# Forgetting-attention decay and mask added on VectorE instead of TensorE; sample output computed with the probabilities stationary, its jobs moved inside the latent-attention heads

## The reference

```python
def _fox_block(q, fq, qpos, k, v, fk, kpos):
    logits = jnp.einsum('bqhd,bkhd->bhqk', q, k, ...) * FOX_SCALE
    decay = jnp.swapaxes(fq, 1, 2)[..., :, None] - jnp.swapaxes(fk, 1, 2)[..., None, :]
    mask = kpos[None, :] <= qpos[:, None]
    p = jax.nn.softmax(jnp.where(mask, logits + decay, NEG_INF), axis=-1)
    return jnp.einsum('bhqk,bkhd->bqhd', p.astype(v.dtype), v)
...
    F = jnp.cumsum(logf_all, axis=1)
...
    o = o.reshape(B, T, FOX_WIDTH) * jax.nn.silu(gate)
    return x + o @ w_out, (k, v, logf.astype(x.dtype))
...
def _mla_block(qn, qr, qpos, kn, kr, v, kpos):
    logits = (einsum(qn, kn) + einsum(qr, kr)) * MLA_SCALE
    mask = (kpos // CHUNK)[None, :] <= (qpos // CHUNK)[:, None]
    p = jax.nn.softmax(jnp.where(mask, logits, NEG_INF), axis=-1)
    return jnp.einsum('bhqk,bkhd->bqhd', p.astype(v.dtype), v)
```

## Time and profile before

| | us |
|---|---|
| median of 3 runs | 2469.4 |
| lowest and highest | 2463.78, 2470.36 |
| the profiled execution | 2464.83 |
| its span, first to last instruction | 2462.8 |
| mean granted TensorE clock | 0.981 of full speed |
| PE busy | 2320.0 (94%) |
| DVE busy | 1099.7 (45%) |
| ACT busy | 910.0 (37%) |
| POOL busy | 212.9 (9%) |

### The profile page before, as it was taken

One profiled execution on the slowest core, in us unless ns is written; L12 is line 12 of the kernel. 1 busy time (PEld: TensorE's weight loads), 2 busy tenths in 40 slices (PEclk: granted clock), 3 DMA queues, 4 the chain that ended last, 5 costly groups with the idle time before them and its releaser, 6 DMA issues. The chain is left out here.

```text
span 2462.8 us, 34026 instructions
## 1 busy us (share of the span) xinstructions
PE 2320.0 (94%) x12338; PEld 1962.2 (80%) x12338; DVE 1099.7 (45%) x2361; ACT 910.0 (37%) x1947; POOL 212.9 (9%) x189
## 2 busy tenths in 40 slices
PE   3899999999999999999997999997699999997998
PEld 2788888888888888877886978887689989996887
DVE  4244444444444444444223343224566666664322
ACT  5233334434333334343223332224444444443211
POOL 0000000000000000000000000004721111110000
PEclk9999999999999999999999999998999999998999
DMA  2322222222222222223433222223321111113332
GB/s 85 103 87 78 86 86 73 82 86 85 79 86 83 81 86 78 87 78 100 159 99 106 74 90 102 100 88 100 127 92 43 47 51 51 43 40 116 120 119 73
DMA packets 95535, 212.33 MB, mean 86 GB/s; under 512 B 9504, under 2 KB 38432, under 8 KB 94768
## 3 DMA queue, kind: packets, MB, share of 16 engines
q1 hardware_dynamic: 95472, 211.45, 26.8%
HBM read 178.60 MB, written 32.82 MB: 86 GB/s over the span
## 5 line engine op out<-in xcount | busy, mean ns | idle before, releaser
L215 PE MATMUL bank<-b_whi,x_hi 128*128 128x512 f32 x1024 | 414.0, 404 | 12.7 <-DVE b_wlo L198 12.7
L215 PE MATMUL bank<-b_wlo,x_hi 128*128 128x512 f32 x1024 | 401.0, 392 | 0.0
L215 PE MATMUL bank<-b_whi,x_lo 128*128 128x512 f32 x1024 | 400.8, 391 | 0.0
L198 DVE SCALAR_TENSOR_TENSOR b_wlo<-b_raw,g_fox,b_whi 128x512 fp32r<-128x512 f32 x256 | 180.9, 748 | 186.1 <-ACT b_whi L185 186.1
L215 PEld LDWEIGHTS bank<-b_whi,x_hi 128*128 128x128 f32 x1024 | 192.8, 188 | 52.2 <-DVE b_wlo L198 12.8
L185 ACT ACTIVATE b_whi<-b_raw,g_fox 128x512 fp32r<-128x512 f32 x256 | 170.6, 715 | 171.4 <-PE bank L215 157.4
L215 PEld LDWEIGHTS bank<-b_whi,x_lo 128*128 128x128 f32 x1024 | 192.6, 188 | 42.3
L215 PEld LDWEIGHTS bank<-b_wlo,x_hi 128*128 128x128 f32 x1024 | 193.0, 188 | 33.8
L215 PE MATMUL bank<-m_whi,x_hi 128*128 128x512 f32 x320 | 124.9, 390 | 0.8 <-DVE m_wlo L198 0.8
L215 PE MATMUL bank<-m_wlo,x_hi 128*128 128x512 f32 x320 | 124.6, 389 | 0.0
L215 PE MATMUL bank<-m_whi,x_lo 128*128 128x512 f32 x320 | 124.5, 389 | 0.0
(11 more groups left out here) (490 smaller groups left out, 5232.2 us busy)
## 6 DMA issues: line engine op xcount, KB each, us to landing
b_raw<-w_fox SPq DMA_DIRECT2D x128, 512.0 KB, 3.5
m_raw<-w_mla SPq DMA_DIRECT2D x40, 512.0 KB, 3.4
c_raw<-w_out SPq DMA_DIRECT2D x32, 512.0 KB, 3.5
g_raw<-w_out SPq DMA_DIRECT2D x32, 512.0 KB, 3.5
f_raw<-w_ukv SPq DMA_DIRECT2D x16, 512.0 KB, 3.4
queries<-e_q SPq DMA_DIRECT2D x16, 480.0 KB, 3.4
f_q<-queries SPq DMA_DIRECT2D x16, 480.0 KB, 3.4
e_raw<-w_uq SPq DMA_DIRECT2D x16, 384.0 KB, 3.5
```

Source lines behind the costliest of these rows:

```text
L198: op = eng.scalar_tensor_tensor(lo[:, k, :], raw[:, k, :], self.gain[:, K:K + 1], hi32[:, k, :], ALU.mult, ALU.subtract)
L215: op = eng.matmul(out, a, w[:, k, :], start=(first and k == 0 and i == 0), stop=(last and k == self.kk - 1 and i == len(pairs) - 1))
```

## The change: what it does, and its diff

**FoX scores.** The two extra products of each score job go. Block a negates F of all heads (DVE), and stores it in a new DRAM tensor `decay`. For each head, SP loads row h of it into five tiles, each row repeated on all partitions (128, 256, 384 and 512 columns on 128 partitions, 576 columns on 64), and POOL adds the mask to the diagonal part of each. DVE's maximum becomes a `tensor_tensor_reduce`: it adds the decay tile to the scores in PSUM, writes the negated sum back, and keeps the minimum. ACT's exponential takes scale -1. A memset of one element stands ahead of each.

**Sample output, both layers.** v is stored as hi and lo side by side, and so are the transposed sample probabilities. One matmul for each key tile holds hi and lo of the probabilities stationary (128 columns) and moves hi and lo of v (256 columns), so 5 matmuls; the fifth has zeros in the lower 64 rows. The result has four parts: ACT copies the lower 64 partitions out, DVE adds twice and multiplies with the gate as it is, and the new job ont transposes that; ACT copies it to the output. Job gn goes.

**Order.** In FoX: before g, gn, o, on in slots 30, 31, 33, 35; after g, o, on, ont in slots 30, 32, 34, 37. In MLA as in the diff.

```diff
-            dve.wait_ge(f_hi.sem, 3)
-            dve.tensor_tensor(K.B[32:32 + HEADS, :], F[:], K.B[0:HEADS, :].bitcast(F32), ALU.subtract).then_inc(f_lo.sem, 1)
...
+            dve.tensor_scalar(nF[:], F[:], -1.0, None, ALU.mult).then_inc(f_neg.sem, 1)
...
+            sp.dma_start(d["decay"], nF[:]).then_inc(out.sem, 16)
...
-            self.sel.wait(eng, g, 2)
             q = slice(i * P, (i + 1) * P)
             for m, (x, y) in enumerate(three(self.qhi, self.qlo, self.khi, self.klo)):
-                eng.matmul(b[:, 0:n], x[:, q], y[:, 0:n], start=(m == 0), stop=False)
-            eng.matmul(b[:, q], K.ident_b[:, :], K.mask_fox_b[:, :], start=False, stop=False, skip_group_check=True)
-            op = eng.matmul(b[:, 0:n], K.A[:, q], K.B[:, 0:n], start=False, stop=True)
+                op = eng.matmul(b[:, 0:n], x[:, q], y[:, 0:n], start=(m == 0), stop=(m == 2))
...
+        self.decay_masked.wait(eng, g, TT)
+        k = ("s0", "s1", "s2", "s3", "sa", "sb").index(name)
+        eng.memset(self.mark[:, k:k + 1], 0.0)
...
-            eng.tensor_reduce(self.nm[:, i:i + 1], b[:, 0:(i + 1) * P], AX.X, ALU.max, negate=True).then_inc(self.negmax.sem, 1)
+            x = b[:, 0:(i + 1) * P]
+            eng.tensor_tensor_reduce(x, x, self.decay[i][:], -1.0, BIG, ALU.add, ALU.min,
+                                     accum_out=self.nm[:, i:i + 1]).then_inc(self.negmax.sem, 1)
...
+                    if g is not None:
+                        H.negmax.wait(sp, g, TT)
+                    row = d["decay"][bass.ds(h, 1)] if not isinstance(h, int) else d["decay"][h:h + 1]
+                    for i in range(NT):
+                        n = (i + 1) * P
+                        sp.dma_start(H.decay[i][:], row[:, 0:n].broadcast_to([P, n])).then_inc(H.decay_in.sem, 16)
+                    sp.dma_start(H.decay_new[:], row[:, SEQ:].broadcast_to([NEW, SAMP])).then_inc(H.decay_in.sem, 16)
...
             def head(g):
...
-                pool.tensor_copy(K.A[0:64, :], K.nsel[0:64, bass.ds(g, 1)].broadcast_to([64, SEQ + NEW])).then_inc(H.sel.sem, 1)
...
+                H.decay_in.wait(pool, g, TT)
+                for i in range(NT):
+                    x = H.decay[i][:, i * P:]
+                    pool.tensor_tensor(x, x, K.mask_fox[:], ALU.add).then_inc(H.decay_masked.sem, 1)
...
                 H.var.wait(pool, g, 1)
                 pool.tensor_tensor(H.rstd[:], H.ss[:], H.half[:], ALU.pow).then_inc(H.rst.sem, 1)
...
         elif name == "on":
+            self.v_lo.wait(eng, g, TT)
             for t in range(TT):
-                n = rows(t)
-                for m, (x, y) in enumerate(three(self.vhi, self.vlo, *self.ptn)):
-                    op = eng.matmul(b[:, 0:256], x[0:n, NT + t, :], y[0:n, t * NEW:t * NEW + 256],
-                                    start=(t == 0 and m == 0), stop=(t == SM and m == 2))
+                op = eng.matmul(b[:, 0:256], self.ptn[:, t, :, :].rearrange("p a q -> p (a q)"),
+                                self.v[:, NT + t, :, :].rearrange("p a d -> p (a d)"), start=(t == 0), stop=(t == SM))
...
+            self.on_moved.wait(eng, g, 1)
+            src = b[0:NEW, 0:256].rearrange("p (a d) -> p a d", a=2)
+            self.release(eng.tensor_tensor(self.on_sum[:], src, self.on_lo[:], ALU.add), name)
+            self.wait_out_of(eng, g, name)
+            eng.tensor_tensor(self.on[:], self.on_sum[:, 0, :], self.on_sum[:, 1, :], ALU.add).then_inc(self.on_added.sem, 1)
+            self.on_added.wait(eng, g, 1)
+            eng.tensor_tensor(self.on[:], self.on[:], self.gate[0:NEW, SM, :], ALU.mult).then_inc(self.on_added.sem, 2)
...
     ORDER = ["qn", "kp", "qr", "T0", "T1", "s3", "ka", "T2", "s2", "new", "T3", "s1", "s0", "T8", "sa", "sb", "T4",
-             "p3", "T5", "p2", "p1", "p0", "T6", "pn", "g", "gn", "T7", "on", "o"]
+             "p3", "T5", "pn", "p2", "p1", "T6", "on", "p0", "g", "T7", "ont", "o"]
```

More of the change, by code:

```diff
@@ L305, in block_a @@
     F = place("a_F", [HEADS, TIME])
+    nF = place("a_nF", [HEADS, TIME])
     T = Transposer(c, "a", x, act, K.ident, KT)
@@ L310, in block_a @@
     wf_hi, wf_lo, f_mm, f_mv, f_sum = c.sem("a_wf_hi"), c.sem("a_wf_lo"), c.sem("a_f_mm"), c.sem("a_f_mv"), c.sem("a_f_sum")
-    soft, logs, scan, f_hi, f_lo, f_t, f_tc, out = (c.sem(f"a_{n}") for n in
-        ("soft", "logs", "scan", "f_hi", "f_lo", "f_t", "f_tc", "out"))
+    soft, logs, scan, f_neg, f_t, f_tc, out = (c.sem(f"a_{n}") for n in
+        ("soft", "logs", "scan", "f_neg", "f_t", "f_tc", "out"))
     with nc.Block() as block:
@@ L371, in _ @@
             act_.activation(e[:], e[:], ACT.Exp).then_inc(soft.sem, 1)
-            act_.wait_ge(soft.sem, 3)
+            act_.wait_ge(soft.sem, 1)
             act_.activation(e[:], e[:], ACT.Ln, bias=K.one_col[0:HEADS, :]).then_inc(soft.sem, 1)
[L375 to L379, removed]
         @block.vector
@@ L803, in pe_job @@
                 op = eng.transpose(b[:, t * P:(t + 1) * P], self.gate[:, t, :], K.ident[:, :])
-        elif name == "gn":
-            op = turn(eng, b[:, 0:NEW], self.gate[0:NEW, SM, :], K.ident[0:NEW, 0:NEW], True)
+        elif name == "ont":
+            self.on_added.wait(eng, g, 3)
+            op = turn(eng, b[:, 0:NEW], self.on[:], K.ident[0:NEW, 0:NEW], True)
         self.end(op, name)
@@ L1953, in pe_job @@
                 f = self.first[j]
-                for m, (x, y) in enumerate(three(self.vhi, self.vlo, *self.pt[j])):
-                    op = eng.matmul(b[:, f:], x[:, j, :], y[:, :], start=(j == 0 and m == 0), stop=(j == NT - 1 and m == 2))
+                for m, (x, y) in enumerate(three(self.v[:, j, 0, :], self.v[:, j, 1, :], *self.pt[j])):
+                    op = eng.matmul(b[:, f:], x, y[:, :], start=(j == 0 and m == 0), stop=(j == NT - 1 and m == 2))
         elif name == "on":
+            self.v_lo.wait(eng, g, TT)
             for t in range(TT):
-                n = rows(t)
-                for m, (x, y) in enumerate(three(self.vhi, self.vlo, *self.ptn)):
-                    op = eng.matmul(b[:, 0:256], x[0:n, NT + t, :], y[0:n, t * NEW:t * NEW + 256],
-                                    start=(t == 0 and m == 0), stop=(t == SM and m == 2))
+                op = eng.matmul(b[:, 0:256], self.ptn[:, t, :, :].rearrange("p a q -> p (a q)"),
+                                self.v[:, NT + t, :, :].rearrange("p a d -> p (a d)"), start=(t == 0), stop=(t == SM))
         elif name == "g":
@@ L1983, in act_job @@
             self.act_exp(eng, g, name)
[L1984 removed]
+        elif name == "g":
             self.wait_ready(eng, g, name)
[L1986 to L1987 removed]
+            self.release(eng.activation(self.gt[:], self.bank(name)[:, :], ACT.Copy), name)
+        elif name == "on":
+            self.wait_ready(eng, g, name)
+            src = self.bank(name)[NEW:2 * NEW, 0:256].rearrange("p (a d) -> p a d", a=2)
+            eng.activation(self.on_lo[:], src, ACT.Copy).then_inc(self.on_moved.sem, 1)
+        elif name == "ont":
+            self.wait_ready(eng, g, name)
+            self.release(eng.activation(dst[:, g, SEQ:], self.bank(name)[:, 0:NEW], ACT.Copy), name)
     def act_exp(self, eng, g, name):
@@ L2358 @@
     "queries": [HEADS, P, TT, BR],
+    "decay": [HEADS, TIME],
 }
```

205 lines of the change are left out of this document (102 added, 103 removed).

## The result

The changed kernel takes 2389.8 us (median of four runs, 2388.5 to 2391.0) where the kernel before, on the same chip, takes 2467.6 us (2463.8 to 2470.4): ratio 0.9686, 95% interval 0.9669 to 0.9702. The prediction was 2392 us. Its profiled execution took 2390.8 us with a span of 2389.1 us, 74.0 us less than the profiled one of before.

The account below looks back on a forecast made before the run. PE bounds both layers, block b wholly. FoX scores 27.0 + FoX output 25.3 + MLA output 22.7 - 0.5 = 74.5 us off the profiled 2464.83 gives 2390.3, from the median 2394.9; stated 2392 us, range 2380 to 2415 (8 in 10).

Parts of the forecast that it names:

- PE bounds both layers: Blocks b and f: PE is the limit (400.00 of 400 us, 294.33 of 300), so matmuls removed are time saved.
- FoX scores, 1.69 us a head: FoX score jobs: six decay products and five masks leave PE, saving 1.69 us per head, 27.0 us for 16 heads.
- FoX sample output, 1.58 us a head: FoX job on: five 256-column matmuls take 0.60 instead of 2.07 us, saving 1.58 us per head, 25.3 in all.
- 49.0 were due: Start of b to start of c, with the FoX jobs of 15 heads: predicted change -49.0 us.
- Block a, put at 0: End of block a: copies and subtractions traded for one negation and one store; cost 0, with 2 us either way.
- Its bare chain: Last FoX head: no slots follow the sample output to cover its chain before ont, costing +0.5 us, once.
- the same four steps: Between FoX on and ont: ACT's copy and three DVE operations, needing some 1.5 us, hidden in other heads.
- MLA, 1.58 - 0.16 = 1.42 us a head: Block f: sample output saves 1.58 us per head, kp's wait grows by 0.16; net 22.7 us for 16 heads.
- The chain foreseen: MLA head's end: f_wlo holds DVE until 2.85 us behind T7's end, delaying DVE's start on o and lengthening kp's wait.
- Decay rows: Block b: five loads per head, 784 KB, land by 567 and masks end about 569, 8 us before POOL's power; cost 0.
- The rival that hands back 26 us: Chains with little room hand part back, in block b's norm and MLA's o: 2418 us, chance 14%.
- the 15 us named: Block b, within the 14% rival: ACT's copy or POOL's masks push the norm chain by 1 us, 15 us come back.

Follow-up runs that it names:

- the scores alone: Kernel before, with only FoX decay and mask moved to DVE (decay rows, `tensor_tensor_reduce`), both sample outputs as they were: 2434.8 us, ratio 0.9874.
- MLA alone: Changed kernel with blocks a and b as before, so only MLA's sample output and job order changed: 2441.4 us, ratio 0.9899 to the kernel before.

## Why the prediction was right

**PE bounds both layers.** Right. A gain of the size of PE's lost busy time, DVE's 32 us added for nothing, and each wait put in front of PE costing its length or more: all three say it.

**FoX scores, 1.69 us a head.** 1.74 by the run with the scores alone. The reading of distances between starts, the next slot's matmul included, held within 0.05.

**FoX sample output, 1.58 us a head.** 1.54 by difference. The new five matmuls take 0.59 us (0.60 said), and the matmul behind them has its usual distance (0.24), as said.

**The first pass and the last head.** The pass of head 0 and the jobs of 15 heads gave 48.6 us where 49.0 were due. The first pass is 0.6 us longer (63.1 us before, 63.7 after); it takes 63.8 in the kernel with MLA alone, whose blocks a and b are those of before, so most of this isn't the change's. Its own part is a wait of 0.1 us for the norm in front of the first transposition. Block a, put at 0, takes 70.0 us before and 69.8 after. The last head is the step that was mis-sized: its pass beside c's first slots takes 64.0 us before and 63.4 after, 0.6 less and not 2.8. Its bare chain was put at 0.5 us, though the prediction gives the same four steps 1.5 us a few sentences earlier; PE waits 1.7. Another 0.9 us stand between c's first matmul and that head's first transposition (12.2 us before, 13.2 after), where PE does the same work. In the changed kernel the granted clock is lower there, 0.78 over 14 us where it was 0.88 (before, then after):

```profile
1090.00:1104.00 14.00, 13.57 (x53) 10.87 (x54) 11.20 (x25) 6.65 (x12) 2.26 (x1) 0.88 0.31 96
1041.00:1055.00 14.00, 13.36 (x48) 10.58 (x49) 11.41 (x25) 6.50 (x13) 2.34 (x1) 0.78 0.32 96
```

Both follow a wait of 4.47 us of PE at the end of the pass before. The kernel with MLA alone takes 12.7 us there, the one with the scores alone 11.9, so this part too differs from kernel to kernel with the clock, for no cause that the runs show.

**MLA, 1.58 - 0.16 = 1.42 us a head.** 1.48 from head to head, and 24.1 us for the block where 22.7 were said. The chain foreseen is there, in PE's and DVE's timeline of a head's end, which answers to the earlier trace rows:

```profile
1962.09 1.23 DVE L195 TENSOR_TENSOR f_wlo<-f_raw,f_whi 128x1024 fp32r<-128x1024 f32 x1
...
1963.37 0.69 DVE L2082 TENSOR_TENSOR o_mla<-bank,f_gt 128x512 f32 x1
...
1964.20 0.65 PE L1948 MATMUL bank<-ident,f_k 128*128 128x128 f32 x4 [0.63 <-DVE o_mla L2082]
```

The split of the next weights ends at 1963.32 and DVE starts on o at once, 2.80 us behind T7's end at about 1960.57 (2.85 said). kp's wait grew from 0.5 to 0.6 us, not to 0.68, and o waits for nothing.

**Decay rows.** The landing was the least certain step. They are all there 10.0 us behind the first issue in the head shown (8.7 to 10.7 over the 16 heads), and the prediction said 8; 4.6 us were left there of the 8 it counted, and in the first head 0.3. The sum didn't change, but the margin was thin: with the masks 2 us in the way each head loses 2.9, and with the loads one place later the gain is gone. The prediction weighed a rule of the Trainium skill (DMA: Bandwidth & Descriptors, Rules for kernel authors), by which a leading zero-stride broadcast of fewer than 16 copies confines a DMA to few engines. These loads have 64 and 128 copies, and the trace agrees that they aren't confined to one: 256 KB in 6.7 us, where one of 16 engines would need 28, an estimate from the earlier trace rows. No run here has fewer than 16 copies.

**What was under-priced: the rivals.** The rival that hands back 26 us was worked out with a wait costing its own length. In three kernels it cost 1.3 to 1.6 times that, because the clock falls behind it. Had the chain in block b been 1 us late, more than the 15 us named could have come back. The forecast was right in spite of it, since no such wait arose in the loops of the changed kernel.

**The total.** 74.5 us were said, and the span is 73.7 us shorter. That the two lie within 1 us is partly luck: the last FoX head gave 2.2 us less and the first pass 0.6 less, MLA gave 1.4 more, and stretches with the same code differ by a few us between kernels. The terms per head, 3.27 and 1.42 against 3.28 and 1.48, are not luck.

## What to carry to other kernels

Where PE is busy for all of a stretch, count what an edit takes from it by the distances between starts, the matmul behind included, and ask of every other engine only whether its result comes in time. A short product that PE adds to a score (a mask, a rank-few bias) is cheap to hand to the engine that reads the scores anyway, if that engine has room, as DVE had here. The order of jobs is priced by its bare chains: a chain of four short operations on two other engines left PE waiting for 1.7 us at the end of FoX, and for 3.2 us in an MLA head, where the split of the next weights stood ahead of it on DVE. Which bank a job takes decides who waits for the last one.

## What the runs showed of the hardware that was not expected

- A wait costs more than its length when the granted clock falls behind it. Around the end of waits of 6.4 to 7.7 us it fell in 15 of 15 heads, behind 3.17 us in 13 of 14 (1.3 us lost each on average), behind 1.84 us in 11 of 15 (1.6 us lost), behind 1.24 us in 6 of 14 (1.5 us lost), and behind the 0.6 us of the changed kernel in none of 15. What decides between waits of one length isn't shown.
- A `tensor_tensor_reduce` with its output in PSUM takes 699 ns for 512 columns, as long as a plain reduction (692 ns), and 142 ns more for the read of the accumulator.
- A matmul of 64 rows among those of 128 costs 0.33 to 0.37 us more than one padded to 128, so that padding with zeros is the faster form.
- Broadcast loads of a DRAM row, five at once and 784 KB, land within 8.7 to 10.7 us of the first issue; one of 256 KB lands in 6.7 us, and a plain load of 512 KB in 3.5.
